# Removing two unused buffers from the SBUF layout of a hybrid decoder layer

## The reference

```python
h    = rmsnorm(x, norm_pre_mix)
proj = h @ w_in                       # 1024 x 4168: f, q, i, g | aq, ak, av | iq, ik, iw
y_a  = hgrn2_mixer(q, f, i, g)        # gated linear recurrence, 4 heads of 128
y_b  = dsa_mixer(aq, ak, av, iq, ik, iw, rel_bias)   # top-128 keys by an indexer, 8 heads of 64
x    = x + rmsnorm(concat(y_a, y_b) @ w_o, norm_post_mix)
h    = rmsnorm(x, norm_pre_ffn)
x    = x + rmsnorm((silu(h @ w_gate) * (h @ w_up)) @ w_down, norm_post_ffn)   # hidden 2816
```

## The kernel before

| Buffer | Start | Start mod 2048 |
|---|---|---|
| hT_hi, hT_lo | 18432, 34816 | 0 |
| raw, w_hi, w_lo | 51200, 67584, 83968 | 0 |
| ident ... rs (small ones) | 100352 to 104608 | - |
| A1 (ff, QK at 131072, w_x at 180224) | 106496 | 0 |
| A2 | 196608 | 0 |

## Time and profile before

### The profile page before, as it was taken

The page is one execution under the profiler, slowest core; times in us unless marked ns, Lnnn a source line. Parts: engine busy times, 40 slices in busy tenths (PEclk is TensorE's granted clock), DMA queues, the critical chain, the costliest instruction groups (busy, mean ns, idle before and its releaser), DMA issues.

```text
span 782.2 us, 9083 instructions
## 1 busy us (share of the span) xinstructions
PE 714.8 (91%) x3744; PEld 611.8 (78%) x3744; DVE 411.2 (53%) x582; ACT 268.3 (34%) x374; POOL 118.5 (15%) x127
## 2 busy tenths in 40 slices
PE   4843999888899999899999999999999999999996
PEld 3832778888898978788879988888888888888885
DVE  4513479987889499774466424433433344221225
ACT  5304455512335282663344313321322213111012
POOL 4300001554412030571021000000000000000001
PEclk9886899999999999799999999999999999999999
DMA  7545311311104413002512512233323333123302
GB/s 246 83 57 117 109 55 54 108 55 55 54 22 134 169 53 109 1 2 108 162 54 81 162 54 67 95 108 108 105 66 99 107 108 107 62 101 108 108 0 107
DMA packets 50512, 69.63 MB, mean 89 GB/s; under 512 B 3592, under 2 KB 42504, under 8 KB 50472
## 3 DMA queue, kind: packets, MB, share of 16 engines
q1 hardware_dynamic: 46512, 60.59, 24.0%
q10 hardware_dynamic: 2312, 2.71, 3.2%
q0 software_dynamic: 1648, 5.77, 2.1%
HBM read 64.35 MB, written 4.72 MB: 88 GB/s over the span
## 4 chain that ended last, share of the span: by engine, by line
PE 69%; DVE 16%; DMA 7%; ACT 4%; issue 2%; POOL 1%; DVEq 0%; SPq 0%; ACTq 0%
PE PS L937 59%; DMA raw<-in_w_in_dram 6%; PE PS L1004 4%; DVE w_lo L639 3%; DVE A L681 2%; PE PS L1098 2%; DVE top L680 2%; DVE A L766 1%; DVE A L765 1%; PE PS L1029 1%; DMA A<-in_x_dram 1%; DVE QK L748 1%; DVE A L789 1%; PE PS L976 1%; DVE hT_lo L643 1%
## 5 line engine op out<-in xcount | busy, mean ns | idle before, releaser
L937 PE MATMUL PS<-hT_lo,w_hi 128*128 128x512 f32 (+2 forms) x584 | 222.9, 382 | 31.5 <-DVE w_lo L639 29.5
L639 DVE TENSOR_TENSOR w_lo<-raw,w_hi 128x2048 fp32r<-128x2048 f32 (+1 forms) x52 | 126.0, 2423 | 199.6 <-ACT w_hi L449 199.3
L937 PE MATMUL PS<-hT_hi,w_lo 128*128 128x512 f32 (+2 forms) x584 | 221.5, 379 | 0.0
L937 PE MATMUL PS<-hT_hi,w_hi 128*128 128x512 f32 (+2 forms) x584 | 221.2, 379 | 0.0
L449 ACT ACTIVATE w_hi<-raw 128x2048 fp32r<-128x2048 f32 (+1 forms) x52 | 98.2, 1889 | 236.6 <-PE PS L937 205.1
L937 PEld LDWEIGHTS PS<-hT_lo,w_hi 128*128 128x128 f32 (+1 forms) x584 | 113.0, 193 | 52.7 <-DVE w_lo L639 28.5
L937 PEld LDWEIGHTS PS<-hT_hi,w_hi 128*128 128x128 f32 (+1 forms) x584 | 113.0, 194 | 20.5 <-issue 0.6
L937 PEld LDWEIGHTS PS<-hT_hi,w_lo 128*128 128x128 f32 (+1 forms) x584 | 113.0, 194 | 18.9 <-issue 0.4
L937 PE MATMUL PS<-w_hi,ff 128*128 128x512 f32 x352 | 108.4, 389 | 0.0
L937 PEld LDWEIGHTS PS<-w_hi,ff 128*128 128x128 f32 x352 | 66.1, 188 | 13.8
L357 POOL TENSOR_SCALAR ms<-ss 128x1 f32<-128x1 f32 (+1 forms) x17 | 7.9, 464 | 452.1 <-ACT raw L623 356.7
(11 more groups left out here) (152 smaller groups left out, 839.3 us busy)
## 6 DMA issues: line engine op xcount, KB each, us to landing
raw<-in_w_in_dram SPq DMA_DIRECT2D x16, 1024.0 KB, 5.6
raw<-in_w_gate_dram SPq DMA_DIRECT2D x11, 1024.0 KB, 5.1
raw<-in_w_up_dram SPq DMA_DIRECT2D x11, 1024.0 KB, 5.1
raw<-in_w_down_dram SPq DMA_DIRECT2D x11, 1024.0 KB, 4.8
raw<-in_w_o_dram SPq DMA_DIRECT2D x4, 1024.0 KB, 4.8
bias_by_distance<-A ACTq DMA_DIRECT2D x1, 2560.0 KB
A<-in_x_dram SPq DMA_DIRECT2D x4, 512.0 KB, 7.9
A<-bias_by_distance POOLq DMA_DIRECT2D x8, 256.0 KB, 4.0
```

Source lines behind the costliest of these rows:

```text
L639: dve.tensor_tensor(lo, view(raw[:, j % 2, :], j), hi.bitcast(F32), ALU.subtract).then_inc(s_lo, 1)
L937: o = pe.matmul(out, lhs[a], rhs[b], start=(first and n == 0), stop=(last and n == 2))
```

## The change

Both unused allocations are deleted. No instruction, operand, shape, semaphore or order differs; every buffer behind the first one starts 1920 bytes lower, and `A1`, its views and `A2` start 3808 bytes lower.

```diff
         PS = ctx.enter_context(nc.psum_tensor("PS", [P, 8, 512], F32))
 
-        sb("front_pad", [P, 480])
         hT_hi = sb("hT_hi", [P, KT, S], F32R)
         hT_lo = sb("hT_lo", [P, KT, S], F32R)
         raw = sb("raw", [P, 2, CH])
@@
         sm = sb("sm", [P, UNITS])
         rs = sb("rs", [P, UNITS])
 
-        sb("middle_pad", [P, 472])
         N1, N2 = FT * 2 * S, 7936
         low = ExitStack()
         A1 = low.enter_context(nc.sbuf_tensor("A1", [P, N1], F32))
```

## The result

| | Before | After |
|---|---|---|
| Median, us | 781.99 (5 runs) | 788.21 (5 runs) |
| Lowest to highest | 781.73 to 784.2 | 787.94 to 789.59 |
| Ratio to before, 95% interval | | 1.008 (1.0067 to 1.0093) |
| Profiled execution: its time, span | 784.2, 782.2 | 787.94, 785.9 |

The kernel is 6.2 us slower; the forecast was 781.9 us and no change, and the range ended at 787.0. The two profiled spans are only 3.7 us apart, because the one of before was the slowest of its runs and the one of after the fastest.

What follows compares the result with a forecast made beforehand. It took TensorE, busy 91% of the span and 69% of the chain, as the bound. Terms of 0 on TensorE, 0 on VectorE and 0 of 3.7 us on DMA left the median at 781.9 us, range 779.0 to 787.0.

Steps and rivals of the forecast that it cites:

- Sum: 0 on TensorE: All TensorE work: the moved addresses were to add 0 us to its matmuls.
- starts at 32 mod 64: TensorE operands in A1, ff, QK, w_x, A2: such starts were to cost 0.
- a crossed 2048-byte line: TensorE's 512-column moving operands reaching into the next line: taken as 0, at most a second 12.6 ns each.
- So no access of another engine or of a DMA delays a read of TensorE here, at whatever distance between the addresses: Feed-forward stretch: an even 226.7 ns cadence beside busy VectorE, ScalarE and DMA was read as no delay.
- ... the loads follow at about 0.23 us. I take 0.: Chunk of 72 columns: weight slices 288 bytes apart, every second at 32 mod 64, were read as costing TensorE 0.
- Going to 160 mod 256 is one unaligned start for another. I take 0 of the 3.7 us.: Bias store on the early chain: its moved source was to cost 0, within 0 to +3.7 us for open transfers.
- A: TensorE's 512-column matmuls: a read crossing a 2048-byte line pays a second 12.6 ns start; 805 us, chance 0.12.
- 375 us or anything over 354: Feed-forward piece of 1608 matmuls: such a time, instead of 351.7 us, was to show crossed lines costing TensorE.
- B: DMA ends off their boundaries, on 57 us of early transfers: up to 6.5%, +3.7 us, 785.6 us; chance 0.15.
- C: Clock falling elsewhere, from 100 to 424 us: up to 11.9 us to regain, taken as -3.4 us, 778.5 us; chance 0.09.
- VectorE at 0: VectorE's 16% of the chain was to stay; line 766 at level 64 to keep 1.22 us.
- The weights' landing at 0: Feed-forward chunks into raw: a 5.1 us landing might become 5.4 us, hidden behind TensorE, so 0.

Runs made afterwards that it cites:

- front_32: Kernel before with hT, raw, w_hi, w_lo and the small tensors 32 bytes further on, A1 and A2 untouched: 787.06 us, ratio 1.0052.
- no_front: Kernel before with only front_pad deleted, so all buffers move down 1920 bytes to 128 mod 2048, distances kept: 782.82 us, ratio 0.9993.
- late_store: Kernel before with the bias store issued at the recurrence's first level, its source in free columns of A2, a wait dropped: 766.98 us, ratio 0.9792.
- store_32: Kernel before with g_sb alone 32 bytes further on, so the bias store reads from 160 mod 256: 784.32 us, ratio 1.002.
- both_32: Kernel before with front_pad 32 bytes longer, all buffers at 32 mod 2048, distances kept: 784.85 us, ratio 1.002.
- rel_256: Kernel after with 96 unused bytes ahead of A1, a distance of 256 mod 512 from the buffers in front: 783.25 us, ratio 1.0004.
- gap_32: Kernel after with 32 unused bytes ahead of A1, which then starts at 320 mod 2048: 786.39 us, ratio 1.0039.
- mid_32: Kernel before with middle_pad 32 bytes longer: A1, ff, QK, w_x and A2 at 32 mod 2048: 788.6 us, ratio 1.0065.
- w_32: Kernel before with w_hi and w_lo alone 32 bytes further on; hT, raw, A1, A2 where they were: 794.84 us, ratio 1.016.
- rel_512: Kernel after with 352 unused bytes ahead of A1, a distance of 512 mod 2048 from the buffers in front: 782.96 us, ratio 0.9993.
- front_128: Kernel before with front_pad gone and middle_pad 952 columns: hT, raw, w_hi, w_lo at 128 mod 2048, A1 and A2 unmoved: 787.47 us, ratio 1.0054.
- ff_32: Kernel before with ff alone 32 bytes further on in its own buffer, A2 64 bytes on: 787.96 us, ratio 1.0056.

## Why the prediction was wrong

**The step that failed: "Sum: 0 on TensorE".** I had listed under "What the change does" that against the front group A1 and ff move by 1888 bytes, and then gave this no price: TensorE got a term for starts at 32 mod 64 and one for a crossed 2048-byte line, both 0, and both were right (front_32, no_front). The relation between TensorE's own two operands got none. The one sentence on distances, "So no access of another engine or of a DMA delays a read of TensorE here, at whatever distance between the addresses", speaks of other engines, and the row behind it could not cover TensorE itself: in the feed-forward stretch of before every distance between its two operands is a multiple of 256 bytes, as slices, halves and blocks are a multiple of 512 bytes long and the two pads kept the buffers so. The even cadence showed one point of a curve. The missing term measured 3.86 us in the gapless stretch. One of the two chunks in w_x, of `w_o`, lies ahead of it: 48 matmuls at the same 6.7 ns would be 0.3 us.

**"... the loads follow at about 0.23 us. I take 0."** I read these rows too coarsely. From the load at 69.94 to that at 71.77 us there are 8 steps: 228.8 ns each (1 ns either way, as the view has hundredths of a us), where 226.7 is the aligned cadence. With slices 288 bytes apart seven of eight are off a multiple of 256 bytes from the moving operand, and in late_store, where the whole chunk runs at full clock, its 23 steps have a mean of 232 ns. This was a hint that something costs here, and no more: the steps do not sort by slice, and the first slice, at a distance of 0, is as slow there as the others. After, `ff`'s loads keep 188 ns while the matmuls come 6.7 ns later, so a load's duration could not have shown the cost.

**The bias store: "Going to 160 mod 256 is one unaligned start for another. I take 0 of the 3.7 us."** Wrong by 1.4 us (store_32); both_32 has 1.8 us with the store at the same start, and the two intervals overlap. A start at 128 mod 256 costs this transfer nothing against 0 mod 256 (below). The bounds 0 to 3.7 us held.

**Sum:** 3.9 + 0.3 + 1.4 to 1.8 = 5.6 to 6.0 us of the measured 6.2 (5.2 to 7.3 by the interval). The 0.3 is an estimate; the other terms are measured.

**The rivals.** A (a crossed line) had the right engine and the wrong cause, with 18.7 us for the 3.86 that the piece shows: 12.6 ns on 1488 matmuls, where 576 pay 6.7; no_front crosses every line and costs nothing. The sign I gave for A, a piece of "375 us or anything over 354", was met at 355.57 by another cause, so it could not tell the two apart. B was right in kind, with 1.4 to 1.8 of its 3.7 us, and by itself within the 0.3%. C (the clock) has no part in the 3.86 us, which arise at a granted clock of 1.00 in both kernels. VectorE at 0 was right: 411.2 us busy before, 411.1 after, and 1.22 us in line 764. The weights' landing at 0 was right: 5.1 us in both kernels, and no_front, with `raw` at 128 mod 256, loses no time.

The Trainium skill's rule (DMA: Bandwidth & Descriptors, "How a descriptor splits into AXI transactions") counts 36 beats for 32 for a kilobyte from such a start, which would be 12.5%. Writes into `raw` do not show it: from 440 to 600 us their queue has a share of 31.2% in no_front and 31.0% before. For the store's source the rule counts 80 beats from 0 mod 256, 84 from 128, 85 from 160 and 86 from 192. The runs agree that a start off 256 can cost, and not on where: 128 is no slower than 0, and 160 is slower than 192 (below). My +1 us by that rule for the first loads was also too much for x: 4096 bytes from 32 mod 256 are 129 beats for 128, an estimate of 0.06 us on 7.58.

## What to carry to other kernels

In a TensorE-bound loop of fp32r matmuls with 512 moving columns, keep the moving and the stationary operand a multiple of 256 bytes apart within the partition; starts at 32 and 128 mod 256 cost TensorE nothing then. (Of other widths only 256 columns were tried, and no other format.) An unused buffer may hold such a distance: rel_256 keeps the time of before with 96 unused bytes instead of 3808. And measure a matmul's price by the spacing of starts, or by the count in a window without gaps; the duration of a record (389 ns at a spacing of 226) is not its price, and that of a weight load did not move.

## What was not expected of the hardware

- Matmuls of 512 columns on fp32r pay 6.7 ns (226 to 233) where the distance of their operands' buffers is 32, 160 or 224 mod 256, 5.7 ns at 128, 2 to 3 ns at 192, nothing at 0. Matmuls of 256 columns pay nothing (24 of them in 2.84 us for 2.87).
- The direction counts, in one kernel at least. In gap_32 the 48 matmuls of `w_o` that move w_x over weights from hT are 192 mod 256 apart the other way round, that is 64 from the moving to the stationary operand; their starts are 233 ns apart in the trace, and those of the 528 on ff 229 ns.
- Which reads meet is open: the moving operand with its own weights' load, or with the next one's. The trace has seven or eight matmuls of each mixed kind, between the projection and the indexer. With weights of their own at 0 and the next one's off (mid_32, front_32) they are 231 to 234 ns apart, for 227 to 228 before, which points to the next one's; but in w_32 seven with only their own off, and seven with neither off, have 232 ns too.
- The store's pace goes by its source's start: 0 and 128 mod 256 are alike, 192 is slower and 160 slowest. From 26 to 62 us, starts at 0 gave 718 or 719 packets (no_front, rel_512, rel_256) and 128 gave 717 or 718 (front_128, front_32, w_32; 713 before); 192 gave 705 and 707 in gap_32 and ff_32; 160 gave 693 to 696 in after, mid_32, both_32 and store_32. The chunk behind the small one follows this pace: its split starts at 74.20 to 75.09 us in the six at 717 to 719, at 76.39 to 76.80 us in the four at 160. The small chunk does not: it lands 43.1 us after its issue in those four, 41.6 or 41.7 us at a source start of 128, and again 43.0 to 43.3 us at 0, which stays unexplained. The queue in no_front, gap_32 and both_32:

```profile
q10 hardware_dynamic: 718, 1.84, 46.6%
```

```profile
q10 hardware_dynamic: 705, 1.80, 47.1%
```

```profile
q10 hardware_dynamic: 696, 1.78, 47.1%
```
